# Down projection ahead of the pooling layer: its last two row blocks, the residual branch, the norm and the map taken in two halves of the tokens, with the squares added by GpSimd

## The reference, cut to what matters

```python
def rmsnorm(x, g):
    y = x * rsqrt(mean(x * x, axis=-1, keepdims=True) + 1e-6)
    return y * g

# second block; u is the normed input of the feed-forward of its layer 0
h = h + rmsnorm(swiglu(u, w_gate, w_up, w_down), g0[3])   # branch
u = rmsnorm(h, g1[0])                                     # norm
m = mixer_pool(u, w_groups, scale)
h = h + rmsnorm(m, g1[1])

def mixer_pool(h, w_groups, scale):
    # four groups of 256 channels: trailing mean over 2/4/8/16 positions
    # minus the token itself, then a 256x256 map per group, then a scale
```

## Time and profile before

| what | value |
|---|---|
| time, median of 3 runs | 1675.54 us (1675.13 to 1675.62) |
| span of the profiled execution, first to last instruction | 1673.3 us |
| time of the profiled execution itself | not listed; median and span differ by 2.2 us |
| PE busy | 1639.8 us, 98% |
| DVE, ACT, POOL busy | 879.9, 706.2, 166.0 us (53, 42, 10%) |
| last matmul of `down_b0` starts | 1252.33 us |
| first matmul with the band matrix starts | 1281.23 us |
| mean granted TensorE clock | 0.994 of full |

### The profile page before, as it was taken

One profiled execution on the slowest core, in us unless ns is written; L12 is line 12 of the kernel. 1 busy time (PEld: TensorE's weight loads), 2 busy tenths in 40 slices (PEclk: granted clock), 3 DMA queues, 4 the chain that ended last, 5 costly groups with the idle time before them and its releaser, 6 DMA issues.

```text
span 1673.3 us, 22206 instructions
## 1 busy us (share of the span) xinstructions
PE 1639.8 (98%) x8041; PEld 1355.4 (81%) x8041; DVE 879.9 (53%) x1443; ACT 706.2 (42%) x1179; POOL 166.0 (10%) x249
## 2 busy tenths in 40 slices
PE   8999999999999999999899999999999999999997
PEld 7777788888888887888777888888888788888887
DVE  5644667777733356666746444443228644444233
ACT  4555554444432236676746332332226532233231
POOL 2011000000000123444402000002000200000001
PEclk9999999999999999999999999999999999999999
DMA  5211222233233342121122333233331132223331
GB/s 181 87 39 50 83 91 92 100 100 100 92 97 101 96 116 68 39 67 60 39 65 75 101 100 99 89 100 101 91 98 51 55 96 100 94 94 96 102 104 51
DMA packets 57157, 144.86 MB, mean 87 GB/s; under 512 B 14160, under 2 KB 20976, under 8 KB 57088
## 3 DMA queue, kind: packets, MB, share of 16 engines
q1 hardware_dynamic: 55680, 141.58, 26.6%
q0 software_dynamic: 688, 1.26, 0.4%
q10 hardware_dynamic: 720, 1.10, 0.2%
HBM read 138.67 MB, written 2.10 MB: 84 GB/s over the span
## 4 chain that ended last, share of the span: by engine, by line
PE 92%; ACT 3%; DVE 3%; issue 1%; POOL 0%; DVEq 0%; ACTq 0%; POOLq 0%
PE ps L1829 26%; PE ps L1830 26%; PE ps L1831 26%; PE ps L2000 1%; PE ps L2239 1%; PE ps L2292 1%; PE ps L2254 1%; PE ps L2240 1%; PE ps L1936 1%; PE ps L1935 1%; PE ps L1934 1%; PE ps L1990 1%; PE ps L2386 0%; PE ps L2078 0%; PE ps L2053 0%
## 5 line engine op out<-in xcount | busy, mean ns | idle before, releaser
L1829 PE MATMUL ps<-hhi,whi 128*128 128x512 f32 x1400 | 553.3, 395 | 2.6 <-DVE wlo L1237 2.1
L1830 PE MATMUL ps<-hlo,whi 128*128 128x512 f32 x1400 | 546.7, 390 | 0.0
L1831 PE MATMUL ps<-hhi,wlo 128*128 128x512 f32 x1400 | 546.4, 390 | 0.0
L1237 DVE TENSOR_TENSOR wlo<-raw,whi 128x1024 fp32r<-128x1024 f32 x234 | 286.6, 1225 | 476.5 <-ACT whi L773 473.7
L773 ACT ACTIVATE whi<-raw 128x1024 fp32r<-128x1024 f32 x247 | 261.2, 1058 | 543.5 <-PE ps L1831 543.1
L1829 PEld LDWEIGHTS ps<-hhi,whi 128*128 128x128 f32 x1400 | 263.7, 188 | 65.9 <-issue 8.2
L1831 PEld LDWEIGHTS ps<-hhi,wlo 128*128 128x128 f32 x1400 | 263.7, 188 | 55.8
L1830 PEld LDWEIGHTS ps<-hlo,whi 128*128 128x128 f32 x1400 | 263.8, 188 | 53.6 <-issue 1.2
L1829 PE MATMUL ps<-ahi,whi 128*128 128x512 f32 x480 | 186.7, 389 | 0.0
L1830 PE MATMUL ps<-alo,whi 128*128 128x512 f32 x480 | 186.7, 389 | 0.0
L1831 PE MATMUL ps<-ahi,wlo 128*128 128x512 f32 x480 | 186.7, 389 | 0.0
(11 more groups left out here) (345 smaller groups left out, 1880.0 us busy)
## 6 DMA issues: line engine op xcount, KB each, us to landing
raw<-w_up_b SPq DMA_DIRECT2D x88, 512.0 KB, 3.4
raw<-w_up_a SPq DMA_DIRECT2D x44, 512.0 KB, 3.5
raw<-w_in_b SPq DMA_DIRECT2D x23, 512.0 KB, 3.7
raw<-w_in_a SPq DMA_DIRECT2D x19, 512.0 KB, 3.5
raw<-w_down_b SPq DMA_DIRECT2D x16, 512.0 KB, 3.4
raw<-w_out_a SPq DMA_DIRECT2D x8, 512.0 KB, 3.5
raw<-w_down_a SPq DMA_DIRECT2D x8, 512.0 KB, 3.5
raw<-w_out_b SPq DMA_DIRECT2D x8, 512.0 KB, 3.5
```

The lines of the kernel that those rows point to most:

```text
L1237: dve.tensor_tensor(wlow(n), raw[n % RAW][:, :], whigh(n).bitcast(f32), ALU.subtract).then_inc(lo_done, 1)
L1829: pe_.matmul(out, wh, hi, start=start, stop=False)
L1830: pe_.matmul(out, wh, lo, start=False, stop=False)
L1831: return pe_.matmul(out, wl, hi, start=False, stop=stop)
```

## The change

The last two rows of `down_b0` are now computed in halves, as those of `down_b1` are. The branch and the norm behind it run twice over the eight rows, at 256 columns each time: once for the first half of the tokens, once for the second (`handover` of ACT and DVE). The operand of the pooling layer's map goes into `ahi` and `alo` in place of `hhi` and `hlo`, and `zt` lies behind it; the second unit of the map's weights goes into free pieces of `alo`. The squares of x are no longer added by PE, row by row: GpSimd adds them over the eight rows of a half (7 additions of 128x256), and PE sums the result over the partitions once per half (`token_sum`). The map runs in two halves (`linear(half, g)`), and so do the tiles of `zt`. The idle matmuls ahead of and behind the sum of `down_b0` are gone. In the diff, lines that only rename counts are left out.

```diff
-        ("norm", 4), ("gemm", "up_b0"), ("gemm", "down_b0"), ("post", 5), ("norm", 6), ("gemm", "pool"),
+        ("norm", 4), ("gemm", "up_b0"), ("gemm", "down_b0"), ("gemm", "pool"),
...
+IN_HALVES = ["down_b0", "down_b1"]
...
-FED = {4: "up_b0", 6: "pool", 8: "up_b1"}
+FED = {4: "up_b0", 8: "up_b1"}
...
+        Z_ORDER = [(half, g) for half in range(2) for g in range(NPOOL)]
+        ACT_Z = {(0, 0): 0, (0, 1): 2, (0, 2): 2, (0, 3): 2, (1, 0): 2, (1, 1): 0, (1, 2): 2, (1, 3): 0}
...
+                for half in range(2):
+                    total = hx[:, 0, HALVES[half]]
+                    for m in range(1, KD):
+                        pool.wait_ge(bsq_ready, KD * half + m + 1)
+                        if m >= 2:
+                            pool.wait_ge(squares_sum, (KD - 1) * half + m - 1)
+                        pool.tensor_tensor(total, sq[:, 0, HALVES[half]] if m == 1 else total, sq[:, m % 2, HALVES[half]],
+                                           ALU.add).then_inc(squares_sum, 1)
...
+                elif n in END_LAST:
+                    act.wait_ge(unit_done, END_LAST[n])
+                elif n == POOL_0:
+                    act.wait_ge(unit_done, FIRST["down_b0"] + END_UNIT + 1)
+                elif n == POOL_1:
+                    act.wait_ge(half_done, HALF_BASE["down_b0"] + 2)
...
+            def half_row(p, m, half):
+                q = m + 2 * half
+                if q < KD + 1:
+                    act.wait_ge(half_done, HALF_BASE[p] + q - END_ROWS[0] + 1)
+                else:
+                    act.wait_ge(unit_done, FIRST[p] + COUNT[p])
+                act.wait_ge(sq_used, sq_base[p] + q - 1)
+                src = ps[:, END_BANK[m, half], HALVES[half]]
+                act.activation(sq[:, q % 2, HALVES[half]], src, ACT.Square).then_inc(sq_ready, 1)
+                act.activation(half_tile(mt, m, half), src, ACT.Copy).then_inc(evac[p], 1)
...
+            def handover():
+                p = "down_b0"
+                def rooted(half):
+                    act.wait_ge(ms_ready, 5 + half + 1)
+                    act.activation(rstd[:, HALVES[half]], ps[:, BANK_MS, HALVES[half]], ACT.Ln, bias=epsc[:, 0:1]
+                                   ).then_inc(rstd_ln, 1)
+                    act.wait_ge(rstd_ln, 5 + half + 1)
+                    act.activation(rstd[:, HALVES[half]], rstd[:, HALVES[half]], ACT.Exp, scale=-0.5
+                                   ).then_inc(rstd_ready, 1)
+                def token_root(half):
+                    cols = slice(2 * half, 2 * half + 2)
+                    act.wait_ge(tok_ready, half + 1)
+                    act.activation(rcol[:, cols], ps[:, BANK_TOK, cols], ACT.Ln, bias=epsc[:, 0:1]).then_inc(rcol_ln, 1)
+                    act.wait_ge(rcol_ln, half + 1)
+                    act.activation(rcol[:, cols], rcol[:, cols], ACT.Exp, scale=-0.5).then_inc(rcol_ready, 1)
+                def applied(m, half):
+                    act.wait_ge(x_done, X_BASE[5] + KD * half + m + 1)
+                    act.activation(half_tile(ahi, m, half), half_tile(x, m, half), ACT.Copy, scale=col(GAIN[6], m)
+                                   ).then_inc(h_hi, 1)
+                    if m >= 2:
+                        act.wait_ge(squares_sum, (KD - 1) * half + max(m - 2, 1))
+                    act.activation(sq[:, m % 2, HALVES[half]], half_tile(x, m, half), ACT.Square).then_inc(bsq_ready, 1)
+                half_row(p, 6, 0)
+                half_row(p, 7, 0)
+                split_hi(POOL_0, 0)
+                rooted(0)
+                for m in range(KD):
+                    applied(m, 0)
+                    if m == 2:
+                        half_row(p, 6, 1)
+                    if m == 4:
+                        split_hi(POOL_1, 0)
+                half_row(p, 7, 1)
+                token_root(0)
+                rooted(1)
+                z_out(0, 1)
+                for m in range(KD):
+                    applied(m, 1)
+                    if m < 2:
+                        z_out(0, 2 + m)
+                    if m in (3, 5):
+                        split_hi(FIRST["pool"] + 2 + (m == 5), 0)
+                token_root(1)
+            def z_out(half, g):
+                act.wait_ge(rcol_ready, half + 1)
+                act.wait_ge(*map_done(half, g))
+                for b in range(2 * half, 2 * half + ACT_Z[half, g]):
+                    act.activation(zt[:, b, g * GW:g * GW + GW], ps[:, Z_BANK[g][half], (b % 2) * GW:(b % 2) * GW + GW],
+                                   ACT.Copy, scale=rcol[:, b:b + 1]).then_inc(B["zc_act"], 1)
...
-                for m in range(KD if e == 6 else 0):
-                    act.wait_ge(x_done, 8 * POSTS.index(e - 1) + m + 1)
-                    act.activation(tile(hhi, m), tile(x, m), ACT.Copy, scale=col(GAIN[e], m)).then_inc(h_hi, 1)
-                    if m >= 2:
-                        act.wait_ge(bsq_used, 7 * BOUNDARY.index(e) + m - 1)
-                    act.activation(sq[:, m % 2, :], tile(x, m), ACT.Square).then_inc(bsq_ready, 1)
-                    if m in (3, 5):
-                        split_hi(FIRST["pool"] + 2 + (m == 5), 0)
...
+            def half_summed(p, m, half):
+                q, cols = m + 2 * half, HALVES[half]
+                dve.wait_ge(sq_ready, sq_base[p] + q + 1)
+                dve.wait_ge(sq_used, sq_base[p] + q)
+                dve.tensor_tensor(sumsq[:, cols], sumsq[:, cols], sq[:, q % 2, cols], ALU.add).then_inc(sq_used, 1)
...
+                def half_lower(m, half):
+                    dve.wait_ge(h_hi, H_BASE[6] + KD * half + m + 1)
+                    dve.scalar_tensor_tensor(out=half_tile(alo, m, half), in0=half_tile(x, m, half), scalar=col(GAIN[6], m),
+                                             in1=half_tile(ahi, m, half).bitcast(f32), op0=ALU.mult, op1=ALU.subtract
+                                             ).then_inc(h_lo, 1)
+                def half_post(m, half):
+                    y = half_tile(mt, m, half)
+                    dve.scalar_tensor_tensor(out=y, in0=y, scalar=col(GAIN[5], m), in1=rstd[:, HALVES[half]],
+                                             op0=ALU.mult, op1=ALU.mult).then_inc(post_done, 1)
                     if m >= 1:
-                        lower(e + 1, 8 * APPLIED.index(e + 1), m - 1)
-                    if m < KD:
-                        dve.wait_ge(post_done, base + m + 1)
-                        dve.tensor_tensor(tile(x, m), tile(x, m), tile(mt, m), ALU.add).then_inc(x_done, 1)
+                        half_lower(m - 1, half)
+                    dve.wait_ge(post_done, X_BASE[5] + KD * half + m + 1)
+                    dve.tensor_tensor(half_tile(x, m, half), half_tile(x, m, half), y, ALU.add).then_inc(x_done, 1)
+                half_summed(p, 6, 0)
+                half_summed(p, 7, 0)
+                split_lo(POOL_0, 0)
+                for half in range(2):
+                    dve.wait_ge(rstd_ready, 5 + half + 1)
+                    dve.wait_ge(evac[p], KD + 2 * half)
+                    if half:
+                        clear_sum("pool")
+                    for m in range(KD):
+                        half_post(m, half)
+                        if half == 0 and m == 3:
+                            half_summed(p, 6, 1)
+                    half_lower(KD - 1, half)
+                    if half == 0:
+                        split_lo(POOL_1, 0)
+                        half_summed(p, 7, 1)
+                        dve.wait_ge(rcol_ready, 1)
+                        z_out(0, 0)
+            def z_out(half, g):
...
             def pool_layer():
                 p = "pool"
+                handover()
                 split_lo(FIRST[p] + 2, 0)
-                clear_sum(p)
                 dve.tensor_tensor(gscale[:, :], vec[:, VEC["pool_scale"]:VEC["pool_scale"] + KD],
                                   vec[:, VEC[GAIN[7]]:VEC[GAIN[7]] + KD], ALU.mult).then_inc(B["gscale"], 1)
-                dve.wait_ge(rstd_ready, RSTD_OF[p] + 1)
+                dve.wait_ge(rcol_ready, 2)
                 for g in range(NPOOL):
...
+                    z_out(1, g)
+                split_lo(FIRST[p] + 3, 0)
...
                             if g % WU == 0:
                                 pe_.wait_ge(lo_done, n0 + g // WU + 1)
                             if half and g == KF * END_ROWS[0] + 6:
-                                mean(0)
+                                half_mean(p, 0)
                             last = block(g, ps[:, END_BANK[m, half], HALVES[half]], HALVES[half], g == KF * m,
                                          g == KF * m + KF - 1)
-                        last.then_inc(half_done, 1)
-                mean(1)
+                            if half and g % WU == WU - 1:
+                                last.then_inc(unit_done, 1)
+                        if half == 0 or m == END_ROWS[0]:
+                            last.then_inc(half_done, 1)
+                if p == ENDING:
```

(98 more changed lines are left out.)

140 lines of the change are left out of this document (53 added, 87 removed).

## The result

The changed kernel takes **1690.42 us** (median of 4 runs, 1689.83 to 1690.9) against 1675.38 for the kernel before in the same session: ratio 1.0085, 95% interval 1.0072 to 1.0098. That is 15.0 us slower, and it lies outside the range that was forecast. The profiled execution spans 1688.3 us, also 15.0 more than before. The kernel before was measured again beside the experiments: 1675.87 us beside the late band, the idle matmuls before the band and in the maps, and the squares on TensorE; 1676.05 beside the other three. Ratios, and differences to the kernel before, are taken within a session; a difference between kernels of two sessions is good to some 0.7 us.

The account below looks back on a forecast made before the run. The prediction took the DVE and ACT row loop to bound PE. Band at 1281.45, plus 0.6, less 1281.23 before, gave +0.8; against the median of 1675.54 that made 1676.3 us, range 1669.8 to 1679.0.

Parts of the forecast that it names:

- Parts 1 to 3: `down_b0` in halves: PE ends 2.2 us later; row loop at 256 columns: 1.40 a row; GpSimd adding squares: pitch 1.95.
- The GpSimd term: Row loop: GpSimd's addition makes DVE's next addition to x wait, 0.55 us a row, bounds 0 and 0.73.
- The rival that it costs nothing: Row loop: GpSimd's additions don't delay DVE, pitch 1.40, time 1669.2 to 1671.2 us, most likely 1670; chance 0.25.
- Part 4: Timing of both halves through token sums, maps, root and `zt`: band matmuls at 1281.45, plus 0.6 for slow PE.
- the tail at half clock: Last nine map matmuls 0.8 us dearer, a band row up to 1.2 more; bounds 0 and 2.0, taken as 0.6.
- its row loop of DVE and ACT: Before the band: high part, low part and addition to x as a serial ring, 2.16 us a row, bounding PE.
- Half clock into the band rows: First band rows at half clock, each 1.2 us dearer; with three slow rows 1679 to 1680 us; chance 0.12.

Follow-up runs that it names:

- the late band: Kernel before, with TensorE waiting ahead of its first band row until ScalarE has made 12 needless copies: 1696.53 us, ratio 1.0124.
- the other three: Changed kernel without 16-column matmuls: 1676.5 us; with squares on TensorE plus idle matmuls: 1672.19 us; with VectorE operands in PSUM plus idle matmuls: 1668.74 us.
- the operands in PSUM: Changed kernel, GpSimd's additions kept, 1/rms and scaled product in PSUM, idle matmuls in TensorE's waits: 1668.74 us, ratio 0.9961 to the kernel before.

## Why the prediction was wrong

Forecast was 1676.3 (no change); it is 1690.42. Places are given behind the first half row, the prediction's from its 1222.6; its 0.6 for the tail is counted ahead of the band.

| step | predicted | measured |
|---|---|---|
| PE's last half row done | 32.1 | 32.1 |
| DVE's first product | 19.8 | 19.8 |
| pitch with GpSimd's additions | 1.95 | 1.95 |
| x of row 7, half 0 | 33.9 | 33.8 |
| first token sum starts | 35.5 | 35.5 |
| DVE starts half 1 | 40.2 | 41.3 |
| x of row 7, half 1 | 54.7 | 56.1 |
| first band matmul | 59.5 | 61.7 |
| band rows and statistics beside before | 0 | +12.7 |

**Parts 1 to 3 held to a tenth.** The GpSimd term, 0.55 a row, was right in mechanism, price and place. The rival that it costs nothing falls with the 0.97 rows. What its 12 rows cost is shown best by the operands in PSUM, at the same level throughout: 5.5 us earlier at the band (52.7 against 58.15). With TensorE adding the two row loops are 5.1 shorter together. Both are less than 12 x 0.55 = 6.6, since a row of 1.40 uncovers ACT's extra work (1.65), as the rival had said. The Trainium skill's rule cited there (SBUF — State Buffer, Who interferes with whom) is borne out in kind: the wait goes away with the second SBUF operand. With the full 0.73 a row it would have been 0.18 a row too dear.

**Part 4 was short by 2.2 us before the band.** The first 12 maps ran at the half level as taken, but so did the sum over partitions (1.05 instead of 0.6), and behind it all was 1.1 to 1.4 late. The tail from x of row 7 to the band took 5.55 at the half level and 4.29 with idle matmuls: that is 1.3, inside the bounds of 0 to 2.0 of which I took 0.6.

**The step that failed** is the last term of the sum, the tail at half clock: "Bounds 0 and 2.0; I take 0.6", so the slow maps and about one slow band row at most. The runs showed eight slow band rows and a slow stage behind them, 12.7 us from the first band matmul to the Ln. With the waits filled, 16.1 us come back (1690.42 - 1674.35), where the sum had 1.1 and 0.6 for the level.

**Behind it stands a reading of the kernel before.** The prediction took its row loop of DVE and ACT for what bounds PE up to the last row, and put the work taken off PE ("64 small pieces of squares and the idle matmuls") at nothing on the path. The chain of the kernel before says otherwise: from 1261.69 to the band it lies on PE itself, and 6.4 us of it are squares. PE was behind its own work and never waited, and from 1265.7 on it stood at the full level. That the squares were on the old path costs the sum nothing, since the new path was added up from its own start. But the change turned a PE that never waits there into one that waits five times between the maps of the second half and for 1.5 us ahead of the band, and that had no price beyond the bounds above.

Which part of the old work was the cover is not shown. With the squares back on PE the maps kept the full level, yet the wait ahead of the band was still there and the band went at half; in the old kernel 24 maps fill that place. The old idle matmuls (from 1252.56 and 1254.75) were not put back by themselves.

**The rival that won was sized by a wrong row.** Half clock into the band rows had 0.12, two or three slow rows at 1.2 each, 1679 to 1680. Its mechanism is what happened, its size was eight rows at 1.43 and the statistics. I argued against more from the earlier trace rows: half clock had lasted 3.5 us of steady work. But those were 256-column matmuls. PE's busy column is the same 100% in both stretches and does not tell the kinds of work apart. In the run without 16-column matmuls the band stage behaved as I had assumed for all of it (back after 3.8 us); with them it was not back in 23.9 us. The forecast should have bounded the case by all eight rows, 8 x 1.4, since no row showed the level return during band rows.

The Trainium skill (TensorE: Matmul & The Clock Gate, What's actually happening) ties the level to how busy TensorE has been. Read with the busy column of the profile, one would expect the rows to get their level back; 23.90 of 23.90 us busy at 0.50 speaks against reading it so.

What stays open: whether it is the short matmuls themselves or the load of new weights before each of them that keeps the level down. They were only taken away together.

## What to carry to other kernels

Before a change takes work off TensorE or gives it new waits, ask which stage it enters next and at what level. Look at whether TensorE waited there before at all: in this kernel the band rows, entered at the half level, did not get it back by themselves. Bound such a case by the whole stage, not by its first rows. Long unread matmuls laid into the waits ahead of the stage can hold the level: here 12, 20 and 5 of them were worth 16 us. And when GpSimd is given work beside VectorE's loop, see which operations of VectorE read two tensors of SBUF; once VectorE's additions to x read one of their two inputs from PSUM, the same GpSimd additions no longer held them up, which was worth 5.6 us here (1674.35 to 1668.74).

## What the runs showed of the hardware

- The granted clock stayed at 1.2 GHz for 37.5 us (1273.7 to 1311.2), and in the last 27.7 of them PE was 100% busy: 23.9 in rows of 128- and 16-column matmuls, then 3.8 with matmuls of 512 columns. The same rows entered at 2.4 GHz kept it (12.6 us in the run with idle matmuls). The old kernel, made to wait 8.2 us, fell to the lower level and stayed there for all eight rows.
- Without the 16-column matmuls the level was back 3.8 us after the first band matmul.
- In one case the fall came 1.0 us into a wait ahead of the band (at 1276.7, when TensorE added the squares), after 16 us at the full level with PE busy for 1.5 to 2.0 of every 2.0 us.
- One-column matmuls are not free on PE: for two blocks of tokens 0.44 us between half rows, though they compute one column each.
- VectorE's addition of 256 columns takes 0.42 alone, 0.97 beside a GpSimd addition of 0.73 when both its inputs are in SBUF, and 0.415 when one is in PSUM.
- It goes the other way too: a GpSimd addition of 0.74 took 1.01 when it started 0.06 us behind a VectorE operation with two inputs in SBUF.
